# A hybrid attention and mixture-of-experts block on one core: order of the expert weights' loads, quad 0's gate and up products in two passes, place of alpha*x1

## The reference

```python
h = (silu(einsum('td,edf->tef', xt, w_gate))      # w_gate, w_up: 32 x 1024 x 256
     * einsum('td,edf->tef', xt, w_up)
     * combine[..., None])                        # two nonzero of 32 for each token
ffn = einsum('tef,efd->td', h, w_down)            # w_down: 32 x 256 x 1024
x = layer_norm(alpha * x1 + ffn, ln2_g, ln2_b)
```

## Time and profile before

| | us |
|---|---|
| median of 3 runs | 436.94 (436.87 to 439.67) |
| the profiled execution, its time | 436.95 |
| its span, first to last instruction | 435.2 |
| TensorE matmuls busy | 374.5 (86% of the span) |
| VectorE busy | 162.6 (37%) |
| ScalarE busy | 131.7 (30%) |
| chain that ended last, share of TensorE | 50% |
| chain that ended last, share of DMA | 29% |

### The profile page before, as it was taken

How to read it: one execution, slowest core, us unless ns; L and a number is a source line. 1 busy time by engine, 2 the same in 40 slices (tenths; PEclk the granted TensorE clock), 3 DMA queues, 4 the chain that set the end, 5 groups by cost and what they waited for, 6 DMA issues and landing times.

```text
span 435.2 us, 6918 instructions
## 1 busy us (share of the span) xinstructions
PE 374.5 (86%) x2737; PEld 271.3 (62%) x2737; DVE 162.6 (37%) x334; ACT 131.7 (30%) x225; POOL 11.8 (3%) x34
## 2 busy tenths in 40 slices
PE   7889899999999999995989559579399397499994
PEld 7789898988999999994545215225235153154543
DVE  3444677775455545546722002002002011021216
ACT  4244455544534444345212102102103031021110
POOL 3000000000000000010010000000000000000004
PEclk9999999999999999997999959869879799599999
DMA  8889884646467675979089999999999999999922
GB/s 287 230 292 363 295 289 168 244 161 211 148 212 261 188 265 178 375 302 379 3 291 424 421 420 418 422 419 421 419 419 418 419 421 419 420 413 420 339 94 96
DMA packets 54505, 134.75 MB, mean 310 GB/s; under 512 B 6608, under 2 KB 39376, under 8 KB 42704
## 3 DMA queue, kind: packets, MB, share of 16 engines
q1 hardware_dynamic: 53904, 132.29, 80.4%
q0 software_dynamic: 576, 2.10, 1.2%
HBM read 133.33 MB, written 1.05 MB: 309 GB/s over the span
## 4 chain that ended last, share of the span: by engine, by line
PE 50%; DMA 29%; DVE 9%; SPq 4%; ACT 3%; issue 2%; POOL 1%; DVEq 0%; POOLq 0%; ACTq 0%
DMA dn<-in_w_down 27%; PE bank L961 21%; PE bank L1204 9%; PE bank L1078 5%; PE bank L1177 3%; PE bank L1154 3%; PE bank L1055 3%; SPq L355 2%; PE bank L1211 2%; DVE wl L645 2%; DMA raw<-in_w_in 2%; SPq L328 1%; ACT wh L495 1%; PE bank L1123 1%; PE bank L969 1%
## 5 line engine op out<-in xcount | busy, mean ns | idle before, releaser
L645 DVE TENSOR_TENSOR wl<-raw,wh 128x1024 fp32r<-128x1024 f32 x56 | 68.3, 1224 | 69.2 <-ACT wh L495 69.0
L961 PE MATMUL bank<-xh,wh 128*128 128x256 f32 x288 | 82.9, 288 | 3.8 <-ACT qT L540 2.6
L961 PE MATMUL bank<-xl,wh 128*128 128x256 f32 x288 | 81.5, 283 | 0.0
L961 PE MATMUL bank<-xh,wl 128*128 128x256 f32 x288 | 81.4, 283 | 0.0
L495 ACT ACTIVATE wh<-raw 128x1024 fp32r<-128x1024 f32 x56 | 58.7, 1056 | 66.8 <-PE bank L961 32.5
L1204 PE MATMUL bank<-dn,hT 128*32 128x512 f32 x256 | 40.5, 790 | 38.4 <-DMA dn<-in_w_down 38.4
L961 PEld LDWEIGHTS bank<-xh,wh 128*128 128x128 f32 x288 | 55.2, 192 | 6.5 <-issue 4.8
L1177 PE MATMUL bank<-gu,xg 128*32 128x512 f32 x512 | 56.6, 594 | 0.0
L961 PEld LDWEIGHTS bank<-xl,wh 128*128 128x128 f32 x288 | 55.2, 192 | 0.2 <-issue 0.2
L961 PEld LDWEIGHTS bank<-xh,wl 128*128 128x128 f32 x288 | 55.2, 192 | 0.0
L1204 PEld LDWEIGHTS bank<-dn,hT 128*32 128x32 f32 x256 | 10.2, 139 | 62.5 <-issue 62.1
(11 more groups left out here) (184 smaller groups left out, 418.2 us busy)
## 6 DMA issues: line engine op xcount, KB each, us to landing
gu<-in_w_gate SPq DMA_DIRECT2D x32, 1024.0 KB, 15.2
gu<-in_w_up SPq DMA_DIRECT2D x32, 1024.0 KB, 17.2
dn<-in_w_down SPq DMA_DIRECT2D x28, 1024.0 KB, 18.3
raw<-in_w_in SPq DMA_DIRECT2D x40, 512.0 KB, 4.8
raw<-in_w_o SPq DMA_DIRECT2D x8, 512.0 KB, 4.8
dn<-in_w_down SPq DMA_DIRECT2D x8, 512.0 KB, 8.3
raw<-in_w_out_conv SPq DMA_DIRECT2D x4, 512.0 KB, 3.6
raw<-in_w_out_attn SPq DMA_DIRECT2D x4, 512.0 KB, 4.6
```

Source lines behind the costliest of these rows:

```text
L645: dve.tensor_tensor(wl[:, s, :].rearrange("p (k c) -> p k c", k=KC), raw[:, pair % NRAW, :].rearrange("p (k c) -> p k c", k=KC) [:, :, n % ...
L961: mm = pe.matmul(dst, w[:, k, :], v[:, i, :], start=(i == 0 and w is h and v is high_in), stop=(i == len(ks) - 1 and w is l))
```

## The change

Three edits. SP's order of loads from quad 2 on becomes gates of 2, w_down 1, ups of 2, w_down 2, and then gate/up q, w_down q for q = 3 to 6, gate/up 7, w_down 7 in halves. Each w_down of q still waits for the second product of quad q-1, each gate/up of q for the gate/up product of quad q-2; the loop is written out. The gates of quad 2 wait for a new semaphore, `gate_ps`: in quad 0 alone, TensorE computes all of the gate columns first (8 k, 256 columns), raises `gate_ps`, then all of the up columns. And the adding of alpha*x1 stands behind quad 2 instead of quad 0.

```diff
@@ SP
-            def load_gu(h, q, experts=range(QE)):
-                for e in experts:
-                    for c, src in ((0, wg_v), (1, wu_v)):
+            def load_gu(h, q, experts=range(QE), parts=range(2)):
+                for c in parts:
+                    for e in experts:
                         sp.dma_start(gu[h][:, e, c, :, :],
-                                     src[:, bass.ds(q * QE + e, 1), :, :]).then_inc(gu_in[h], 16)
+                                     (wg_v, wu_v)[c][:, bass.ds(q * QE + e, 1), :, :]).then_inc(gu_in[h], 16)
...
-            def load_quad(h, q, last=False):
-                rounds = through(q - 1)
-                sp.wait_ge(gu_ps, rounds)
-                load_gu(h, q, range(QE // 2) if last else range(QE))
-                sp.wait_ge(y_ps, 2 * rounds)
-                load_dn(q - 1)
-                if last:
-                    load_gu(h, q, range(QE // 2, QE))
-            with sp.Fori(1, NQ // 2 - 1) as o:
-                for h in range(2):
-                    load_quad(h, 2 * o + h)
-            load_quad(0, NQ - 2)
-            load_quad(1, NQ - 1, last=True)
+            over = through(1)
+            sp.wait_ge(gate_ps, over)
+            load_gu(0, 2, parts=[0])
+            sp.wait_ge(y_ps, 2 * over)
+            load_dn(1)
+            load_gu(0, 2, parts=[1])
+            sp.wait_ge(y_ps, 2 * through(2))
+            load_dn(2)
+            def load_quad(h, q):
+                sp.wait_ge(gu_ps, through(q - 1))
+                load_gu(h, q)
+                sp.wait_ge(y_ps, 2 * through(q))
+                load_dn(q)
+            for q in range(3, NQ - 1):
+                load_quad(q % 2, q)
+            sp.wait_ge(gu_ps, through(NQ - 2))
+            load_gu((NQ - 1) % 2, NQ - 1)
             sp.wait_ge(y_ps, 2 * through(NQ - 1))
             for h in range(2):
                 load_dn_cols(h, NQ - 1)
@@ TensorE
-                        for k in range(KC):
-                            if k == KC // 2:
-                                pe.wait_ge(xg_v, c + 1)
-                            for e in range(QE):
-                                g = slice(SLOTS * e, SLOTS * (e + 1))
-                                mm = pe.matmul(bank[6][g, :], xg[:, k, g], w[:, e, :, k, :],
-                                               start=(k == 0), stop=(k == KC - 1))
-                        mm.then_inc(gu_ps, 1)
+                        passes = [slice(0, 1), slice(1, 2)] if q == 0 else [slice(0, 2)]
+                        for part in passes:
+                            for k in range(KC):
+                                if k == KC // 2:
+                                    pe.wait_ge(xg_v, c + 1)
+                                for e in range(QE):
+                                    g = slice(SLOTS * e, SLOTS * (e + 1))
+                                    mm = pe.matmul(bank[6][g, part.start * DE:part.stop * DE], xg[:, k, g],
+                                                   w[:, e, part, k, :],
+                                                   start=(k == 0), stop=(k == KC - 1), skip_group_check=True)
+                            mm.then_inc(gu_ps if part.stop == 2 else gate_ps, 1)
...
-                if q == 0:
+                if q == 2:
                     pe.wait_ge(x1_done, X1_PARTS)
                     seed(True)
```

More of the change, by code:

```diff
@@ L259, in hybrid_block @@
         put_done = sem("put_done")
+        gate_ps = sem("gate_ps")
         gu_ps = sem("gu_ps")
```

## The result

The changed kernel takes 431.76 us (median of 4 runs, 430.95 to 432.57) against 436.98 us: a ratio of 0.9861, 95% interval 0.9832 to 0.9889. It is faster, by 5.2 us or 1.4%, where 4.2 us or just under 1% was forecast. Measured again with the same program (experiment 5) it took 432.21 us against 437.19, so 5.0 us: ratio 0.990 (0.9874 to 0.9926).

The account below looks back on a forecast made before the run. The expert half was taken as bound by one late-starting, never pausing weight stream, then TensorE's tail. Quad 7's second product moving from 418.20 to 414.03 saves 4.2 us: 436.94 becomes 432.8 us, own range 432.1 to 433.5.

Parts of the forecast that it names:

- part 1: Quad 0's gate/up in two passes: first gate load issued at 214.77, 3.54 us earlier, gate pass 0.2 us longer.
- third rival: Quad 0's split exposes its weight loads: gates 1 us later, quad 0's end 0.6 later; 433.6 us, chance 0.16.
- Rival 2: Quad 0's short passes run no faster than long ones, an instruction costing and not a column; 436.3 us, chance 0.08.
- the seed: Adding alpha*x1: left behind quad 0 it would make a hole of 0.4 us in the load stream.
- part 2: New load order from quad 2 on: stream does not run dry, w_down 2 issued at 246.25, margin 3.1 us.
- rival 4: Loads in flight share the stream instead of queuing, so w_downs land late; 47 us more, 484 us, chance 0.04.
- the threshold: Load stream has a hole only if the next issue comes later than the last outstanding landing less 2.4 us.
- part 3: Quad 7: gate/up lands at 402.05, second product starts at 414.0 instead of 418.20, w_down 7 hidden by 1.5 us.
- the clock: Quad 7's gate/up product after idling: low clock costs 1.60 to 2.94 us more, mean 2.28.
- rival 1: Clock stays full in quad 7's gate/up, second half of its second product waits for w_down 7; 431.3 us, chance 0.10.
- the sum: Quad 7's second product starts 418.20 - 414.03 = 4.2 us earlier, the 17.0 us after it unchanged; 432.8 us, chance 0.62.

Follow-up runs that it names:

- experiment 5: Changed kernel again, unaltered; 432.21 us against 437.19 for the kernel before, ratio 0.99, 219.03 us from q0.
- Experiments 1 and 2: First: changed kernel with quad 0's gate/up in one pass again, 436.73 us. Second: kernel before with the two passes and early gate loads alone, 434.08 us.
- experiment 3: Changed kernel with the adding of alpha*x1 behind quad 0 again; 433.76 us, ratio 0.9907 to the kernel before.
- Experiment 11: Changed kernel with 8 filler calls (1.8 us) ahead of quad 1's gate/up product; 433.69 us, ratio 0.9881 to the kernel before.
- experiment 7: Changed kernel with quad 7's gate loads first, on their own semaphore and in their own pass; 430.38 us, ratio 0.9858 to the kernel before.
- its two relatives: Kernel before with SP's loop written out, 224.42 us from q0; kernel before with only the adding of alpha*x1 moved behind quad 2, 224.61 us.
- experiment 12: Kernel of experiment 7 with 10 filler calls between quad 7's two passes; 431.11 us, ratio 0.9828 to the kernel before.
- experiment 9: Changed kernel with 20 filler calls ahead of quad 7's gate/up product; 431.97 us, ratio 0.9845 to the kernel before.
- experiment 6: Changed kernel with 44 filler calls ahead of quad 7's gate/up product; 433.21 us, ratio 0.991 to the kernel before.
- experiments 7 and 8: The second of these: kernel of experiment 7 with w_down 7 in four loads of whole rows; 431.69 us, ratio 0.9885 to the kernel before.

## Why the prediction was right and wrong

**The release (part 1): right.** Quad 0's two passes took 7.11 us against 7.07 for one, so the split cost 0.04 us where 0.2 was taken for the gate pass alone, and the first gate load went out 3.72 us from q0 (3.95 forecast, 7.29 before). Experiments 1 and 2 show its worth from both sides. Without it gate/up 7's product starts 3.1 us later (193.83 against 190.70, the mean of the two profiles) and the end comes 2.8 us later; with it alone the end comes 3.0 us earlier. The timed medians give 4.1 and 3.6. With the 7.11 us of the two passes the third rival, priced at 433.6, is out. The rule of the Trainium skill that stands in part 1 ("TensorE: Matmul & The Clock Gate", Part 3, The mechanism) would have put some 2 us on the two passes; the measurement decides against it for 32-column tiles in the same rows. (The same section of the Trainium skill also lets a load into the background weight buffer go ahead of running matmuls; no run here shows by which way these loads are hidden.) Rival 2, by which two short passes would take twice as long, is out with the same row.

**The order and the seed (part 2): right in kind, the seed undersized.** The loads landed in order of issue (w_down 1 by 240.2 us, ups 2 from 242.7 on), w_down 2 was issued at 245.01 with ups 2 in at 250.5, a margin of 3.1 us as forecast, and rival 4 did not occur. The seed's place was priced at a hole of 0.4 us; it is 1.3 to 1.7 in the stream (experiment 3), since the step took an empty queue to cost only its lateness. Experiment 11 confirms the threshold itself. That does not enter the forecast, which had the seed moved. SP's issues did stall (12.87 us for four loads). The profile's chain counts them (SPq L324 8%), but the stream ran at 414 to 423 GB/s in every slice from the 22nd to the 37th, so no load was late for it.

**The tail (part 3): right in kind.** Gate/up 7's product started at 190.50 and 190.89 from q0 (191.13 forecast), lost 2.6 and 1.6 us to the clock (2.28 forecast; rival 1's full clock did not occur), and the second product started at 202.71 and 202.02 (203.01 forecast). W_down 7 stayed hidden: experiment 7 had to take more than 1 us off TensorE's side to bring it to the path. The same experiment bears out rival 1's statement that w_down 7 would cap a gain from the clock.

**What failed: the sum, and what was made of it.** The step that failed is the last one, 418.20 - 414.03 = 4.2 us. The way to the gain was right and its size too small: the runs gave 5.2 and 5.0 us in the medians and 5.1 from q0. In the sum's own terms the end was forecast at 220.01 from q0 and came at 219.34 (mean of 219.65 and 219.03), and the kernel before, taken at 224.18, lay at 224.40 as the mean of itself and its two relatives. The 0.9 us between 4.2 and 5.1 is made of terms that each erred the same way by 0.2:
- the release: first gate load at 3.72 from q0, not 3.95. The 0.2 put on the gate pass for its weight loads was not there; both passes together cost 0.04.
- the stream, from that issue to the start of gate/up 7's product: 186.8 and 187.2, not 187.2 (402.15 - 214.97).
- the clock: 2.6 and 1.6 lost, 2.1 on average, not 2.28. The prediction took the mean of five losses as if it were the size, though they ran in a row like the one described above (5.98, 6.18, 6.58, then 5.24, 5.63).
- the kernel before: 224.18 in the one profile that the sum was drawn from, 0.2 under the mean of three.

Only the first is shown for itself, as the release lies at 3.72 in both profiles of the changed kernel. The other three are of the size of the scatter between profiles, and dividing the rest among them is arithmetic on two or three executions. No new mechanism is needed.

The second half of the failure is what the chances made of it. By its own words faster by over 1% took rival 1 and the better half of the forecast, so 0.10 and about half of 0.62, some 0.4; the larger part lay within 1%, because the forecast was "just inside". With 4.2 us so close to 4.4, errors of 0.2 in four terms decide the outcome, and nothing in the working spoke for one side. The repeat shows how close it is: 1.0%, interval 0.7 to 1.3%. That the measured 431.76 us lies nearer to rival 1's 431.3 than to the forecast's 432.8 is chance, since rival 1's condition did not occur.

The prediction also read its times from one profiled execution, with quad 0's product at 211.02. In the sum this start cancels, but times such as 414 for quad 7's second product hang on it. Over the fourteen profiles it lies between 209.95 and 212.38, and that scatter, 2.4 us, is half as large as the effect.

## What to carry to other kernels

Where one stream of loads bounds a stage, find what lets the first of its loads go and split the operation that holds it: here 3.3 of 3.4 us came through to the last weights that bound the end, as the queue never ran empty. The limit for every later issue is the last landing in flight less the start-up time (2.4 us here); up to there a delay was free (1.9 us in experiment 11), beyond it a hole cost more than its lateness (1.3 to 1.7 us for 0.3 in experiment 3). Count from an event just ahead of the changed code and not from the start of the span, when effects of 1% are to be read from single profiles.

## What had not been expected of the hardware

- The clock can fall after an idle stretch has ended: 2.16 us idle at granted clock 1.00, then a mean of 0.86 in the first 1.8 us of the next work and 0.50 in the 2 us behind (experiment 12). Idle stretches of 4.36 us (experiment 9) and 7.28 us (the changed kernel) dropped it as well. Only with no gap did quad 7's product run in 7.07 us (experiment 6).
- The loss behind equal waits steps from one to the next: products of 8.55, 8.92, 9.31 and 9.69 us in quads 4 to 7 of the changed kernel, which start 29.9 to 30.0 us apart.
- A queue that ran empty for a moment needed about 3 us to be back at its rate (74, 197, 328 GB/s in successive microseconds, experiment 3).
- With the half rows of w_down 7 in flight the 16 DMA engines were fully busy at 387 to 389 GB/s, with whole rows at 420 (experiments 7 and 8).
